# Expert weights in fewer, larger transfers: four slots of 4 MB in place of eight of 2 MB

## The chip, the core and the metric

The kernel runs on one core of a Trainium2 chip. The metric is the device time of one execution in microseconds; it was 1150.12 us before the change (median of three runs, 1147.99 to 1150.42). All data is float32.

## What is computed

One layer of a decoder trunk on 304 tokens (256 prompt tokens behind 16 meta tokens, and 8 sequences of 4 tokens). A mixer of three head groups comes first, then a mixture of 32 experts, of which each token uses four. Both parts end in a layer norm. The change lies in the experts:

```python
def moe(h, lp):
    logits = (xf @ lp["router_w"] + lp["router_b"]).astype(jnp.float32)
    top_val, top_idx = lax.top_k(logits, TOP_K)            # 4 of 32
    gates = jax.nn.softmax(top_val, axis=-1)
    ...
    def expert_block(args):
        xb, e = args
        hid = xb @ lp["moe_w1"][e] + lp["moe_b1"][e]       # 1024 x 2048 weights, 8 MB
        gate = jnp.minimum(hid[:, :D_FF], SWIGLU_LIMIT)
        lin = jnp.clip(hid[:, D_FF:], -SWIGLU_LIMIT, SWIGLU_LIMIT)
        act = gate * jax.nn.sigmoid(SWIGLU_ALPHA * gate) * (lin + 1.0)
        return act @ lp["moe_w2"][e] + lp["moe_b2"][e]     # 1024 x 1024 weights, 4 MB
    ...
    y = jax.ops.segment_sum(rows, tok, num_segments=n)     # sum with the gates
```

Every expert's weights are read once, 32 x 12 MB = 403 MB of the 424 MB that the kernel reads.

## The kernel before

The mixer runs first, up to about 200 us. Its weights and its tensors lie in one large SBUF tensor, `ring`. Its first 32768 columns are afterwards the ring of expert weights: eight slots (`SLOTS`) of 4096 columns (`SLOT`), 16 KB per partition and 2 MB each. An expert is six pieces (`PIECES`): four of the first layer (`W1P`), each 256 rows of `moe_w1`, and two of the second, each 512 rows of `moe_w2`. In both, one partition's share of a piece is one run of 16 KB in memory: partition p holds rows 2p and 2p+1 of a first-layer piece, or rows 4p to 4p+3 of a second-layer piece. Piece number k of the whole sequence goes to slot k mod 8.

All loads of weights are issued by SyncE (SP) in the order of its program. `load_first` loads the pieces of expert 0's first layer while the mixer still runs; each waits with `filled(sp, freed_by(...))` for the last matmul job that reads the mixer's projection weights in that part of the ring. Between them SP issues the second half of `w_out` and, behind them, the rows of the layer norm (`lnbc`). Then come two pieces of expert 1 in the last slots, and the second layer of expert 0 in slots 4 and 5 when job P11 has read `w_out`, which lies there. With that the ring holds eight pieces, 16 MB. From then on `load_group` (L461 to L475) waits before each load until the slot's old piece has been used (`w_used`), which is counted over all pieces.

TensorE takes the experts in pairs. For an expert of the pair (j is 0 or 1) the first layer is eight blocks k of 128 rows (L1651 to L1664). The tokens are the stationary operand, at most 64 per expert, and the weights are the moving one: four products of 512 columns per block, each two matmul instructions in float32. `slot_of` waits for the piece of a block to have landed (`w_full`), and `w_used` is raised after each piece's last block. In the first expert of a pair half of the gather for the following pair is done ahead of block 3 (`gather(1)`), the other half (`gather(0)`) behind the second expert's first layer. The gather picks the tokens of an expert with matmuls (L1610); its stationary operand is `xt` with a step of two columns, because partition p of a piece holds rows 2p and 2p+1. Behind the first layer come the combine of the pair before (L1618, L1625), the transposes of the activation (L1677), the biases of the next expert (L1565) and the second layer, eight blocks again (L1688 to L1700). VectorE and ScalarE compute the activation and add up the results.

Of the kernel before, what the change touches and what calls it, by code (L numbers as in the profile page):

```python
# [22 lines left out]
P = 128  # L23
D = 1024
# [28 lines left out]
C_Z = C_R + DC  # L53
DIN = C_Z + RANK

PIECES = 6
W1P = 4
SLOTS = 8
GROUP = 4
SLOT = 4096  # L60
MB1 = 2048
CAP = 64
PASSES = -(-TOUT // CAP)
# [44 lines left out]
def build_kernel(nc, x_prompt, x_sample, state_conv_a, state_rglru, state_conv_b, state_gla, meta_tokens, ln0_g, ln0_b,  # L108
# [4 lines left out]
    with ExitStack() as ctx:  # L113
# [11 lines left out]
        xt = sb("xt", [P, 3, D])  # L125
# [140 lines left out]
        pick = part("moe", 3, 2 * CAP)  # L266
# [39 lines left out]
        ld_moe = sem("ld_moe")  # L306
        w_full = [sem(f"w_full{s}") for s in range(SLOTS)]
        w_used = sem("w_used")
# [59 lines left out]
            return 64 * (h % 2), h // 2  # L368

        def w1_piece(e, s):  # L370
            return moe_w1[0, bass.ds(e, 1), s * 2 * P:(s + 1) * 2 * P, :].rearrange("a (p t) c -> p (a t c)", t=2)

        def w2_piece(e, s):
            r = (s - W1P) * 4 * P
            return moe_w2[0, bass.ds(e, 1), r:r + 4 * P, :].rearrange("a (p t) c -> p (a t c)", t=4)

        def slot(s):
            return ring[:, s * SLOT:(s + 1) * SLOT]


        @block.sync
        def _(sp):
# [33 lines left out]
            sp.dma_start(wout[:, 0:4, :], w_out[0, 0:4 * P, :].rearrange("(k p) n -> p k n", p=P)).then_inc(ld_wout[0], 16)  # L416
            w1_order = sorted(range(W1P), key=lambda s: J[freed_by(s * SLOT, (s + 1) * SLOT)])

            def load_first(s):
                filled(sp, freed_by(s * SLOT, (s + 1) * SLOT))  # L420
                sp.dma_start(slot(s), moe_w1[0, 0, s * 2 * P:(s + 1) * 2 * P, :].rearrange("(p t) c -> p (t c)", t=2)
                             ).then_inc(w_full[s], 16)

            for s in w1_order[0:3]:
                load_first(s)
            sp.wait_ge(ya_ready, MA)
            sp.wait_ge(outcols_ready, 2)
            sp.dma_start(wout[:, 4:8, :], w_out[0, 4 * P:8 * P, :].rearrange("(k p) n -> p k n", p=P)).then_inc(ld_wout[1], 16)
            for s in w1_order[3:4]:
                load_first(s)  # L430
            sp.wait_ge(h0_ready, 3)
            sp.dma_start(lnbc[:, 0, :], ln1_g.to_broadcast([P, D])).then_inc(ld_ln, 16)
# [4 lines left out]
            sp.wait_ge(S0_decayed, 2)  # L437
            copied(sp, "ST1")
            for s in range(PIECES, SLOTS):
                r = (s - PIECES) * 2 * P  # L440
                sp.dma_start(slot(s), moe_w1[0, 1, r:r + 2 * P, :].rearrange("(p t) c -> p (t c)", t=2)
                             ).then_inc(w_full[s], 16)
            sp.wait_ge(moe_cleared, 4)
            for b in range(2):
# [1 line left out]
                             ).then_inc(ld_moe, 16)  # L446
            sp.dma_start(eout[0:NE, :, :], moe_b2[0].rearrange("e (h c) -> e h c", h=2)).then_inc(ld_moe, 16)
            filled(sp, "P11")
            for s in range(W1P, PIECES):
                r = (s - W1P) * 4 * P  # L450
                sp.dma_start(slot(s), moe_w2[0, 0, r:r + 4 * P, :].rearrange("(p t) c -> p (t c)", t=4)
                             ).then_inc(w_full[s], 16)
            sp.wait_ge(h1_ready, 3)
            sp.dma_start(lnbc[:, 0, :], ln2_g.to_broadcast([P, D])).then_inc(ld_ln, 16)
            sp.dma_start(lnbc[:, 1, :], ln2_b.to_broadcast([P, D])).then_inc(ld_ln, 16)
# [5 lines left out]
            def load_group(e, n, first=0):  # L461

                for i in range(GROUP):
                    if (i + 1) * PIECES <= first:
                        continue
                    ei = e + i if isinstance(e, int) else sp.snap(e + i)
                    for c in range(PIECES):
                        k = i * PIECES + c
                        if k < first:
                            continue  # L470
                        s = k % SLOTS
                        src = w1_piece(ei, c) if c < W1P else w2_piece(ei, c)
                        dst = slot(s)
                        sp.wait_ge(w_used, PIECES * n + k - SLOTS + 1)
                        sp.dma_start(dst, src).then_inc(w_full[s], 16)  # L475

# [822 lines left out]
        def _(pe):  # L1299
# [299 lines left out]
            for t in range(3):  # L1599
                ins = pe.matmul(bank[4][:, 0:NE], ones[:, :], M[:, t, :], start=t == 0, stop=t == 2)  # L1600
# [3 lines left out]
            def gather(half):  # L1604

                for k in range(4 * half, 4 * half + 4):
                    out = bank[(2, 5)[k // 4]][:, (k % 4) * 2 * CAP:(k % 4 + 1) * 2 * CAP]
                    c = 2 * P * (k // 2) + k % 2
                    for t in range(3):
                        ins = pe.matmul(out, xt[:, t, c:2 * P * (k // 2 + 1):2], pick[:, t, :], start=t == 0, stop=t == 2)  # L1610
                ins.then_inc(gather_full, 1)

            def combine(pi, c):
# [17 lines left out]
            for t in range(3):  # L1631
                ins = pe.transpose(bank[3][0:NE, t * P:(t + 1) * P], gates[:, t, :], ident[:, :])
# [3 lines left out]
            with pe.Fori(0, n_pass) as r:  # L1636
                with pe.Fori(0, NE // GROUP) as g:
                    uses = (r * (NE // GROUP) + g) * (GROUP * PIECES // SLOTS)
                    for q in range(2):
                        pi = r * PAIRS + 2 * g + q  # L1640
                        for j in range(2):
                            n = 2 * pi + j

                            def slot_of(c):

                                k = (2 * q + j) * PIECES + c
                                pe.wait_ge(w_full[k % SLOTS], 16 * (uses + k // SLOTS + 1))
                                return k % SLOTS * SLOT


                            for k in range(KT):  # L1651
                                if j == 0 and k == 3:
                                    gather(1)
                                if j == 0 and k % 4 == 0:
                                    pe.wait_ge(xT_ready, 2 * pi + 1 + k // 4)
                                if k % 2 == 0:
                                    at_ = slot_of(k // 2)
                                for b in range(2):
                                    for h in range(2):
                                        c = at_ + k % 2 * MB1 + (2 * b + h) * 512  # L1660
                                        ins = pe.matmul(bank[b][64 * h:64 * h + 64, :], xT[:, q, k, j * CAP:(j + 1) * CAP],  # L1661
                                                        ring[:, c:c + 512], start=False, stop=k == KT - 1)
                                if k % 2 == 1:
                                    ins.then_inc(w_used, 1)  # L1664

                            if j == 1:
# [9 lines left out]
                            for k in range(4):  # L1676
                                ins = pe.transpose(bank[3][:, k * P:(k + 1) * P], l1[:, k:512:4], ident[:, :])  # L1677
# [4 lines left out]
                            if j == 1:  # L1682
                                pe.wait_ge(put_ready, n + 1)
                                for t in range(3):
                                    ins = pe.transpose(bank[3][:, t * P:(t + 1) * P], put[:, t, :], ident[:, :])
                                ins.then_inc(putT_full, 1)
                                pe.wait_ge(out_ready, 2 * n + 1)
                            for k in range(KT):  # L1688
                                if j == 0 and k == 6:
                                    combine(pi, NCOMB - 1)  # L1690
                                if k % 4 == 0:
                                    at_ = slot_of(W1P + k // 4)
                                for h in range(2):
                                    c = at_ + k % 4 * D + h * 512

                                    a = actT[:, k % 4, (k // 4) * CAP:(k // 4 + 1) * CAP]
                                    ins = pe.matmul(bank[4][64 * h:64 * h + 64, :], a, ring[:, c:c + 512],  # L1697
                                                    start=k == 0, stop=k == KT - 1)
                                if k % 4 == 3:
                                    ins.then_inc(w_used, 1)  # L1700

            pe.wait_ge(putT_ready, n_pass * PAIRS + 1)
            pe.wait_ge(out_ready, n_pass * (4 * PAIRS) + 1)
# [31 lines left out]
```

## Time and profile before

| | |
|---|---|
| median of the runs | 1150.12 us (1147.99 to 1150.42) |
| profiled execution, its time | 1150.01 us |
| its span | 1148.2 us |
| TensorE busy | 1089.9 us, 95% of the span |
| DMA: bytes, mean rate | 425.72 MB, 371 GB/s |
| loads of expert weights issued | 192 of 2048 KB, median 31.5 us from issue to landing |

The page gives busy shares of the whole span and a strip of 40 slices. The strip shows the mixer up to slice 7 (about 200 us) with the DMA engines partly idle, and from slice 9 to slice 38 a constant rate of 426 to 429 GB/s. The instructions' rows name engine, line, operation, the tiles written and read, and the shape. PE is the matmul, PEld the load of the stationary operand, SPq the queue of SyncE.

### The profile page before, as it was taken

How to read it: one execution, taken by the hardware profiler on the slowest of the kernel's cores; microseconds unless marked ns; L12 is line 12 of the kernel's file. 1: busy time of each engine (PE TensorE's matmuls, PEld its weight loads, DVE VectorE, ACT ScalarE, POOL GpSimd, SP SyncE). 2: the span in 40 equal slices, each digit the busy share in tenths (PEclk: the TensorE clock that was granted, in tenths of full speed). 3: DMA queues.
4: the chain of work that ended last, by engine and by line, in shares of the span. 5: the costliest groups of instructions: out<-in, count | busy, mean ns of one | idle time of the engine just before them, and what ended most of it. 6: DMA issues, size and time to landing. Idle time of an engine off the chain costs nothing.

```text
span 1148.2 us, 13702 instructions
## 1 busy us (share of the span) xinstructions
PE 1089.9 (95%) x5399; PEld 477.7 (42%) x5399; DVE 341.0 (30%) x798; ACT 166.2 (14%) x290; POOL 73.5 (6%) x119
## 2 busy tenths in 40 slices
PE   6999899999999999999999999999999999999994
PEld 3666536534444434434344333333333333333331
DVE  3489755322121212121212121212121212121225
ACT  3444122110111011101010101011101110110002
POOL 8401430000000000000000000000000000000000
PEclk9999888899999999999999999999999999999997
DMA  9522845599999999999999999999999999999991
GB/s 311 168 74 74 336 174 197 212 399 428 426 428 428 429 429 429 428 428 429 429 428 429 429 428 428 429 429 429 428 428 428 429 429 428 429 429 428 428 420 44
DMA packets 40700, 425.72 MB, mean 371 GB/s; under 512 B 7073, under 2 KB 11302, under 8 KB 16097
## 3 DMA queue, kind: packets, MB, share of 16 engines
q1 hardware_dynamic: 38761, 423.68, 88.3%
q0 software_dynamic: 1920, 1.80, 0.6%
q8 instruction: 11, 0.18, 0.1%
q14 instruction: 8, 0.07, 0.0%
HBM read 423.50 MB, written 2.17 MB: 371 GB/s over the span
## 4 chain that ended last, share of the span: by engine, by line
PE 68%; DMA 25%; DVE 5%; ACT 1%; issue 1%; SPq 0%; ACTq 0%; DVEq 0%
PE bank L1661 25%; DMA ring<-in_moe_w_dram 25%; PE bank L1697 14%; PE bank L1314 8%; PE bank L1610 7%; PE bank L1625 5%; PE bank L1565 2%; PE bank L1349 1%; PE bank L1677 1%; PE bank L1618 1%; PE bank L1530 1%; DVE ring L1001 1%; PE bank L1395 0%; PE bank L1319 0%; DVE stat L870 0%
## 5 line engine op out<-in xcount | busy, mean ns | idle before, releaser
L1661 PE MATMUL bank<-ring,hT 128*64 128x512 f32 x2048 | 454.2, 594 | 20.4 <-DMA ring<-in_moe_w_dram 19.7
L1661 PEld LDWEIGHTS bank<-ring,hT 128*64 128x64 f32 x2048 | 143.0, 137 | 313.6 <-issue 262.8
L1697 PE MATMUL bank<-ring 128*64 128x512 f32 x1024 | 230.3, 597 | 0.0
L1268 DVE TENSOR_SCALAR ring<-bank 128x512 f32<-128x512 f32 x32 | 22.1, 692 | 372.6 <-PE bank L1661 372.6
L1697 PEld LDWEIGHTS bank<-ring 128*64 128x64 f32 x1024 | 69.2, 137 | 146.6 <-issue 140.1
L1610 PEld LDWEIGHTS bank<-ring,xt 128*128 128x128 f32 x792 | 98.1, 201 | 27.9 <-issue 26.0
L1610 PE MATMUL bank<-ring,xt 128*128 128x128 f32 x792 | 104.3, 290 | 1.8 <-DVE ring L1200 1.8
L1206 DVE COPY hT<-bank 128x512 f32<-128x512 f32 x33 | 22.6, 684 | 258.9 <-PE bank L1610 258.9
L842 ACT ACTIVATE ring<-ring 128x512 f32<-128x512 f32 x32 | 20.2, 630 | 491.5 <-DVE ring L1268 491.5
L851 ACT ACTIVATE ring<-bank 64x512 f32<-64x512 f32 x64 | 37.8, 591 | 243.9 <-PE bank L1697 243.1
L1217 DVE TENSOR_TENSOR ring<-ring,bank 128x512 f32<-128x512 f32 x68 | 43.4, 676 | 87.9 <-PE bank L1625 87.8
L1625 PE MATMUL bank<-ring 128*128 128x512 f32 x136 | 67.2, 617 | 0.0
L648 POOL TENSOR_TENSOR ring<-ring 128x256 f32<-128x256 f32 x1 | 0.7, 719 | 962.2 <-ACT ring L857 962.2
L1314 PE MATMUL bank<-hT,ring 128*128 128x304 f32 (+2 forms) x176 | 47.3, 430 | 3.5 <-DVE hT L904 2.5
L1314 PEld LDWEIGHTS bank<-hT,ring 128*128 128x128 f32 (+1 forms) x176 | 32.2, 184 | 17.9 <-issue 7.6
L1625 PEld LDWEIGHTS bank<-ring 128*128 128x128 f32 x136 | 23.1, 189 | 36.7 <-issue 36.7
L1565 PE MATMUL bank<-ring 32*64 32x512 f32 x264 | 35.9, 613 | 0.0
L1314 PE MATMUL bank<-ring 128*128 128x512 f32 (+1 forms) x92 | 35.3, 542 | 0.0
L1001 DVE SCALAR_TENSOR_TENSOR ring<-ring 128x256 f32<-128x256 f32 x60 | 32.8, 588 | 1.1
L844 ACT ACTIVATE ring<-bank 128x512 f32<-128x512 f32 x32 | 19.1, 597 | 74.8 <-PE bank L1677 74.8
L1314 PEld LDWEIGHTS bank<-ring 128*128 128x128 f32 x92 | 17.3, 190 | 17.0 <-issue 14.9
L1277 DVE TENSOR_SCALAR ring<-io,ring 128x64 f32<-128x64 f32 x96 | 23.9, 300 | 0.0
(290 smaller groups left out, 621.1 us busy)
## 6 DMA issues: line engine op xcount, KB each, us to landing
ring<-in_moe_w_dram SPq DMA_DIRECT2D x192, 2048.0 KB, 31.5
ring<-in_w_out_dram SPq DMA_DIRECT2D x2, 2048.0 KB, 12.2
ring<-in_w_in_dram SPq DMA_DIRECT2D x2, 1536.0 KB, 17.1
ring<-in_w_in_dram SPq DMA_DIRECT2D x1, 3072.0 KB, 24.8
ring<-in_w_in_dram SPq DMA_DIRECT2D x1, 2048.0 KB, 13.6
ring<-in_w_in_dram SPq DMA_DIRECT2D x1, 1600.0 KB, 8.1
lnbc<-in_ln_g_dram SPq DMA_DIRECT2D x3, 512.0 KB, 20.9
lnbc<-in_ln_b_dram SPq DMA_DIRECT2D x3, 512.0 KB, 11.2
```

The costliest lines, as they stand in the source:

```text
L851: act.activation(eout[64 * j:64 * j + 64, h, :], bank[4][64 * h:64 * h + 64, :], ACT.Copy).then_inc(out_ready, 1)
L1001: st.do(dve.scalar_tensor_tensor(uc[:, m, 0:SEQ], src, w, uc[:, m, 0:SEQ], ALU.mult, ALU.add), uc_ready if (k, m) == (WB - 1, MB - 1) else ...
L1206: dve.tensor_copy(xT[:, parity, 4 * b:4 * b + 4, :], bank[(2, 5)[b]][:, :].rearrange("p (k c) -> p k c", c=2 * CAP)).then_inc(xT_ready, 1)
L1217: dve.tensor_tensor(dst, dst, bank[COMB_BANK[c]][:, :], ALU.add).then_inc(y_added, 1)
L1268: dve.tensor_scalar(g1[:, :], bank[0][:, :], LIMIT, None, ALU.min).then_inc(g1_ready, 1)
L1277: ins = dve.tensor_scalar(put[:, t, j * CAP:(j + 1) * CAP], io64[:, :], posm[:, t, bass.ds(n, 1)], gates[:, t, bass.ds(e, 1)], ALU.is_equa ...
L1314: ins = pe.matmul(out, a, b, start=n == 0, stop=n == len(pairs) - 1)
L1565: pe.matmul(bank[b][64 * h:64 * h + 64, :], bsel[e0:e0 + NE, j, :], b1_sb[e0:e0 + NE, h, :], start=True, stop=False)
L1610: ins = pe.matmul(out, xt[:, t, c:2 * P * (k // 2 + 1):2], pick[:, t, :], start=t == 0, stop=t == 2)
L1625: pe.matmul(out[:, :], putT[:, t * P:(t + 1) * P], eout[:, h, :], start=True, stop=True).then_inc(comb_full, 1)
L1661: ins = pe.matmul(bank[b][64 * h:64 * h + 64, :], xT[:, q, k, j * CAP:(j + 1) * CAP], ring[:, c:c + 512], start=False, stop=k == KT - 1)
L1697: ins = pe.matmul(bank[4][64 * h:64 * h + 64, :], a, ring[:, c:c + 512], start=k == 0, stop=k == KT - 1)
```

## The change

An expert is now three pieces of 4 MB: two of the first layer, 512 rows each, and one second layer. The ring has four slots of 8192 columns. In a piece of the first layer partition p holds rows 4p to 4p+3, one run of 32 KB in memory. A second layer is loaded in one transfer with two runs of 16 KB per partition, one from each half. The order of rows in the first layer is another, so the gather's stationary operand is read with a step of four columns. Waits for landing and signals of use follow the larger pieces.

```diff
--- before.py
+++ after.py
@@ -53,11 +53,11 @@
 C_Z = C_R + DC
 DIN = C_Z + RANK
 
-PIECES = 6
-W1P = 4
-SLOTS = 8
+PIECES = 3
+W1P = 2
+SLOTS = 4
 GROUP = 4
-SLOT = 4096
+SLOT = 8192
 MB1 = 2048
 CAP = 64
 PASSES = -(-TOUT // CAP)
@@ -368,11 +368,10 @@
             return 64 * (h % 2), h // 2
 
         def w1_piece(e, s):
-            return moe_w1[0, bass.ds(e, 1), s * 2 * P:(s + 1) * 2 * P, :].rearrange("a (p t) c -> p (a t c)", t=2)
-
-        def w2_piece(e, s):
-            r = (s - W1P) * 4 * P
-            return moe_w2[0, bass.ds(e, 1), r:r + 4 * P, :].rearrange("a (p t) c -> p (a t c)", t=4)
+            return moe_w1[0, bass.ds(e, 1), s * 4 * P:(s + 1) * 4 * P, :].rearrange("a (p t) c -> p (a t c)", t=4)
+
+        def w2_piece(e):
+            return moe_w2[0, bass.ds(e, 1), :, :].rearrange("a (h p t) c -> p (a h) (t c)", h=2, t=4)
 
         def slot(s):
             return ring[:, s * SLOT:(s + 1) * SLOT]
@@ -418,15 +417,15 @@
 
             def load_first(s):
                 filled(sp, freed_by(s * SLOT, (s + 1) * SLOT))
-                sp.dma_start(slot(s), moe_w1[0, 0, s * 2 * P:(s + 1) * 2 * P, :].rearrange("(p t) c -> p (t c)", t=2)
+                sp.dma_start(slot(s), moe_w1[0, 0, s * 4 * P:(s + 1) * 4 * P, :].rearrange("(p t) c -> p (t c)", t=4)
                              ).then_inc(w_full[s], 16)
 
-            for s in w1_order[0:3]:
+            for s in w1_order[0:1]:
                 load_first(s)
             sp.wait_ge(ya_ready, MA)
             sp.wait_ge(outcols_ready, 2)
             sp.dma_start(wout[:, 4:8, :], w_out[0, 4 * P:8 * P, :].rearrange("(k p) n -> p k n", p=P)).then_inc(ld_wout[1], 16)
-            for s in w1_order[3:4]:
+            for s in w1_order[1:2]:
                 load_first(s)
             sp.wait_ge(h0_ready, 3)
             sp.dma_start(lnbc[:, 0, :], ln1_g.to_broadcast([P, D])).then_inc(ld_ln, 16)
@@ -437,8 +436,8 @@
             sp.wait_ge(S0_decayed, 2)
             copied(sp, "ST1")
             for s in range(PIECES, SLOTS):
-                r = (s - PIECES) * 2 * P
-                sp.dma_start(slot(s), moe_w1[0, 1, r:r + 2 * P, :].rearrange("(p t) c -> p (t c)", t=2)
+                r = (s - PIECES) * 4 * P
+                sp.dma_start(slot(s), moe_w1[0, 1, r:r + 4 * P, :].rearrange("(p t) c -> p (t c)", t=4)
                              ).then_inc(w_full[s], 16)
             sp.wait_ge(moe_cleared, 4)
             for b in range(2):
@@ -446,10 +445,8 @@
                              ).then_inc(ld_moe, 16)
             sp.dma_start(eout[0:NE, :, :], moe_b2[0].rearrange("e (h c) -> e h c", h=2)).then_inc(ld_moe, 16)
             filled(sp, "P11")
-            for s in range(W1P, PIECES):
-                r = (s - W1P) * 4 * P
-                sp.dma_start(slot(s), moe_w2[0, 0, r:r + 4 * P, :].rearrange("(p t) c -> p (t c)", t=4)
-                             ).then_inc(w_full[s], 16)
+            sp.dma_start(slot(W1P).rearrange("p (h c) -> p h c", h=2), moe_w2[0, 0].rearrange("(h p t) c -> p h (t c)", h=2, t=4)
+                         ).then_inc(w_full[W1P], 16)
             sp.wait_ge(h1_ready, 3)
             sp.dma_start(lnbc[:, 0, :], ln2_g.to_broadcast([P, D])).then_inc(ld_ln, 16)
             sp.dma_start(lnbc[:, 1, :], ln2_b.to_broadcast([P, D])).then_inc(ld_ln, 16)
@@ -469,8 +466,8 @@
                         if k < first:
                             continue
                         s = k % SLOTS
-                        src = w1_piece(ei, c) if c < W1P else w2_piece(ei, c)
-                        dst = slot(s)
+                        src = w1_piece(ei, c) if c < W1P else w2_piece(ei)
+                        dst = slot(s) if c < W1P else slot(s).rearrange("p (h c) -> p h c", h=2)
                         sp.wait_ge(w_used, PIECES * n + k - SLOTS + 1)
                         sp.dma_start(dst, src).then_inc(w_full[s], 16)
 
@@ -1605,9 +1602,9 @@
 
                 for k in range(4 * half, 4 * half + 4):
                     out = bank[(2, 5)[k // 4]][:, (k % 4) * 2 * CAP:(k % 4 + 1) * 2 * CAP]
-                    c = 2 * P * (k // 2) + k % 2
+                    c = 4 * P * (k // 4) + k % 4
                     for t in range(3):
-                        ins = pe.matmul(out, xt[:, t, c:2 * P * (k // 2 + 1):2], pick[:, t, :], start=t == 0, stop=t == 2)
+                        ins = pe.matmul(out, xt[:, t, c:4 * P * (k // 4 + 1):4], pick[:, t, :], start=t == 0, stop=t == 2)
                 ins.then_inc(gather_full, 1)
 
             def combine(pi, c):
@@ -1653,14 +1650,14 @@
                                     gather(1)
                                 if j == 0 and k % 4 == 0:
                                     pe.wait_ge(xT_ready, 2 * pi + 1 + k // 4)
-                                if k % 2 == 0:
-                                    at_ = slot_of(k // 2)
+                                if k % 4 == 0:
+                                    at_ = slot_of(k // 4)
                                 for b in range(2):
                                     for h in range(2):
-                                        c = at_ + k % 2 * MB1 + (2 * b + h) * 512
+                                        c = at_ + k % 4 * MB1 + (2 * b + h) * 512
                                         ins = pe.matmul(bank[b][64 * h:64 * h + 64, :], xT[:, q, k, j * CAP:(j + 1) * CAP],
                                                         ring[:, c:c + 512], start=False, stop=k == KT - 1)
-                                if k % 2 == 1:
+                                if k % 4 == 3:
                                     ins.then_inc(w_used, 1)
 
                             if j == 1:
@@ -1688,16 +1685,15 @@
                             for k in range(KT):
                                 if j == 0 and k == 6:
                                     combine(pi, NCOMB - 1)
-                                if k % 4 == 0:
-                                    at_ = slot_of(W1P + k // 4)
+                                if k == 0:
+                                    at_ = slot_of(W1P)
                                 for h in range(2):
-                                    c = at_ + k % 4 * D + h * 512
+                                    c = at_ + k * D + h * 512
 
                                     a = actT[:, k % 4, (k // 4) * CAP:(k // 4 + 1) * CAP]
                                     ins = pe.matmul(bank[4][64 * h:64 * h + 64, :], a, ring[:, c:c + 512],
                                                     start=k == 0, stop=k == KT - 1)
-                                if k % 4 == 3:
-                                    ins.then_inc(w_used, 1)
+                            ins.then_inc(w_used, 1)
 
             pe.wait_ge(putT_ready, n_pass * PAIRS + 1)
             pe.wait_ge(out_ready, n_pass * (4 * PAIRS) + 1)
```

## Rows read from the trace of the kernel before

**Rows 1.** the page: busy time, and the chain that ended last, by engine
```profile
PE 1089.9 (95%) x5399; PEld 477.7 (42%) x5399; DVE 341.0 (30%) x798; ACT 166.2 (14%) x290; POOL 73.5 (6%) x119
...
PE 68%; DMA 25%; DVE 5%; ACT 1%; issue 1%; SPq 0%; ACTq 0%; DVEq 0%
```

**Rows 2.** stretches: us, busy PE, PEld, DVE, ACT, POOL, clock, DMA share, GB/s
```profile
213.00:214.00 1.00, 1.00 (x8) 0.21 (x4) 0.00 (x0) 0.00 (x0) 0.00 (x0) 1.00 1.22 229
...
213.00:250.00 37.00, 37.00 (x184) 14.23 (x182) 7.97 (x20) 2.41 (x4) 0.00 (x0) 1.00 0.94 368
...
500.00:600.00 100.00, 100.00 (x504) 39.59 (x502) 22.47 (x51) 10.85 (x18) 0.00 (x0) 1.00 1.01 429
...
600.00:700.00 100.00, 96.77 (x479) 37.31 (x475) 20.05 (x49) 10.06 (x16) 0.00 (x0) 1.00 1.01 428
```

**Rows 3.** timeline of TensorE, two pairs' first lines: start, us, line, operation, count
```profile
543.85 5.32 PE L1661 MATMUL bank<-ring,hT 128*64 128x512 f32 x24
...
573.82 13.90 PE L1661 MATMUL bank<-ring,hT 128*64 128x512 f32 x64
...
599.65 0.60 PE L1661 MATMUL bank<-ring,hT 128*64 128x512 f32 x2
```

**Rows 4.** DMA view of 73 to 75 us (4 KiB runs) and 300 to 1100
```profile
DMA packets 202, 0.83 MB, mean 414 GB/s; under 512 B 0, under 2 KB 0, under 8 KB 202
...
q1 hardware_dynamic: 202, 0.83, 102.5%
...
DMA packets 23536, 342.74 MB, mean 428 GB/s; under 512 B 2617, under 2 KB 2617, under 8 KB 2617
...
q1 hardware_dynamic: 23534, 342.71, 100.6%
```

**Rows 5.** waits of TensorE on weights: total, times, longest
```profile
PE bank L1661 <- DMA ring<-in_moe_w_dram: 19.7, 26, 1.2
```

**Rows 6.** timeline of TensorE at the start of the stream
```profile
209.00 5.37 PE L1661 MATMUL bank<-ring,hT 128*64 128x512 f32 x24 [0.69 <-DVE hT L1206]
...
214.30 3.09 PE L1610 MATMUL bank<-ring,xt 128*128 128x128 f32 x24
...
217.33 8.80 PE L1661 MATMUL bank<-ring,hT 128*64 128x512 f32 x40
...
237.25 1.94 PE L1697 MATMUL bank<-ring 128*64 128x512 f32 x8
```

**Rows 7.** timeline of SP's queue: start, us, line, tile, count
```profile
105.34 14.07 SPq L421 DMA_DIRECT2D ring<-in_moe_w_dram  x3
...
119.53 0.38 SPq L428 DMA_DIRECT2D ring<-in_w_out_dram  x1
...
212.69 40.60 SPq L475 DMA_DIRECT2D ring<-in_moe_w_dram  x10
```

**Rows 8.** timeline of TensorE at the end of the stream
```profile
1106.84 3.65 PE L1661 MATMUL bank<-ring,hT 128*64 128x512 f32 x16 [0.64 <-DMA ring<-in_moe_w_dram]
...
1111.73 3.65 PE L1661 MATMUL bank<-ring,hT 128*64 128x512 f32 x16 [1.24 <-DMA ring<-in_moe_w_dram]
...
1115.32 3.09 PE L1610 MATMUL bank<-ring,xt 128*128 128x128 f32 x24
...
1120.40 7.09 PE L1697 MATMUL bank<-ring 128*64 128x512 f32 x32
```

**Rows 9.** weight loads by line: ns min/median/max, first and last start
```profile
L1610 PEld LDWEIGHTS bank<-ring,xt x792: 192/197/331, 202.6 to 1118.0; 128*128 128x128 f32 x198
...
L1677 PEld LDWEIGHTS bank<-ident,ring x128: 195/209/222, 229.0 to 1118.6; 128*128 128x128 f32 x128
...
L1685 PEld LDWEIGHTS bank<-ident,ring x48: 137/140/143, 257.5 to 1120.1; 128*128 128x128 f32 x48
```

**Rows 10.** timelines of TensorE, VectorE: first uses of w_out, of the norm's rows
```profile
145.45 9.18 PE L1530 MATMUL bank<-ring 128*64 128x512 f32 x32
...
160.81 1.26 DVE L886 SCALAR_TENSOR_TENSOR xt<-xt,mv,lnbc 32x1024 f32<-32x1024 f32 x1
```

## Prediction

> **What bounds the kernel now.** I read the page first: the matmul engine is busy 95% of the span, and the chain that ended last lies 68% on it and 25% on the loads of expert weights [rows 1]. Both numbers are averages over two regimes, so I read the table of stretches next. Between 500 and 600 us TensorE has no idle time at all; between 600 and 700 it is idle for 3.2%; the DMA engines move 428 to 429 GB/s in both [rows 2]. The stream of weights is saturated from about 240 us to the end, and only the lead changes: at 209 us the ring holds 16 MB, TensorE eats a pair of experts in 55.80 us (543.85 to 599.65) [rows 3], and the stream delivers one in 12 transfers of 2 MiB at 342.74 MB in 800 us, 428.4 GB/s [rows 4], 12 x 4.895 = 58.74 us. TensorE gains 2.9 us per pair, so the lead is used up near 600 us. From there it waits for weights, 19.7 us in 26 waits, all in the first layer of an expert [rows 5]. So the end of the kernel is: first issue of the stream, plus what the stream loses at its start, plus the bytes at the stream's rate, plus what TensorE does after the last first-layer transfer has landed. Each edit is costed in these four terms.
>
> **The start of the stream.** Loads are issued when a slot has been used. Before, slot 0 is used after two of eight row blocks (k): the first matmuls start at 209.00 [rows 6], SP issues at 212.69 [rows 7]. After, it is used after four, and between the third and the fourth lies the second half of the gather (214.30, 3.09 us). The fourth block is 8 of the 40 matmuls that take 8.80 us from 217.33 [rows 6], so it ends at 217.33 + 1.76 = 219.09; with the 0.1 us that lay between use and issue before, the first issue is at 219.2, 6.5 us later. Not all of it is lost. Before, the queue ran dry between the small slots: 368 GB/s over the stretch 213 to 250 [rows 2], 13.6 MB. After, traffic begins about 1 us behind the issue (before, 229 GB/s between 213 and 214 is half of the full rate, so traffic began near 213.5 to 213.7) [rows 2], so at 220.2. Two transfers of 4 MiB keep it busy until 220.2 + 2 x 9.79 = 239.8. The second slot is free at 226.2 (the 40 matmuls end at 226.13), in time. The third slot, the whole second layer, is free when its last matmuls end at 237.25 + 1.94 = 239.2 [rows 6], and its load arrives at 240.3: a gap of 0.5 us. The fourth is free 7.04 us later at 246, the next at 253, the one after that when expert 1 ends, 25.83 us after its start (573.82 to 599.65) [rows 3], so at 265; the stream would want them at 250, 260 and 270. So 29.3 us of traffic by 250, 12.55 MB, against 13.6: 1.05 MB or 2.5 us behind. I add 0.5 us for the ramp of the first transfer: **+3.0 us**. Bounds: +2.5 if there is no ramp, +6.5 if none of the old gaps is won back.
>
> **In the steady part** the ring is as large as before (16 MB), so a load waits for a slot only if TensorE is late. A matmul of the first layer takes 0.22 us of TensorE's time (8.80 / 40) [rows 6], four blocks 7.04, an odd expert 25.83 and an even one 55.80 - 25.83 = 29.97 [rows 3]. Transfers of 4 MiB land 9.73 us apart. Count from the landing A of an even expert's first piece: it is used at A + 7.04 + 3.09 = A + 10.1, the second (landed A + 9.7) at A + 17.2, and the expert ends at A + 30.0. The odd one has used its first piece at A + 37.0, waits for the second until A + 38.9, and needs the other 25.83 - 7.04 = 18.8 us from there, so it ends at A + 57.7, before the next pair's first landing at A + 58.4. A piece is used 7 to 11 us after its landing, and the stream wants the slot 27 us after it. So the stream stays saturated, and TensorE waits 2 to 3 us per pair, in fewer and longer waits of up to 1.9 us.
>
> **The rate of the stream.** The one gain. First-layer transfers change from 16 KiB runs to 32 KiB runs; the second layer keeps 16 KiB runs (two per partition). The trace before has no load with 32 KiB runs, so I draw a line through two sizes. With 4 KiB runs (the load of w_out, alone on the queue) it moves 414 GB/s, 4096 x 16 / 414 = 158.3 ns per run and engine; with 16 KiB runs 428.4 GB/s, 611.9 ns [rows 4]. The slope is 453.6 / 12288 = 36.9 ps per byte, which leaves 7.1 ns fixed per run. By the shares of busy time instead (102.5% of 16 engines x 2 us / 202 runs = 162.4 ns; 100.6% x 16 x 800 us / 20,919 long runs = 615.6 ns, less a little for the short packets) it is near 11 [rows 4]. I take 8, nearer the first, because shares over 100% count overlap. 92 transfers follow after the prefetch, 61 of the first layer; each of these saves 8 runs per engine, 488 in all, and 92 of the short packets that end a transfer vanish (2617 short packets in 800 us, 16 per transfer [rows 4]), which I count like a fixed part. 580 x 8 ns = **-4.6 us**. Bounds: 0 and 580 x 11 = -6.4.
>
> The Trainium skill, DMA: Bandwidth & Descriptors, section on where 436 GB/s comes from, puts the limit of the ports at 435.2 GB/s. The slope above is 434 GB/s over 16 engines, so the trace agrees. At that limit the 256 MB of the first layer would go 9.3 us faster, an end that no run length can pass.
>
> **The end.** The last transfer of the first layer lands one second layer's worth (4 MiB, 9.8 us) before the stream ends, as before. Then TensorE worked off two blocks (1111.73 to 1115.32, 3.6 us); now it has four, 7.04 us: +3.45 us. Behind it nothing moves: gather, transposes and biases until the second layer at 1120.40, 5.1 us [rows 8]. The second layer is now waited for whole, but it lands 9.8 us after the first layer's last piece and is wanted 12 us after it, so that wait is hidden; it would cost 3.5 us if the first layer were faster than 4.7 us there.
>
> **The gather** now reads its stationary operand with a step of 16 bytes, before 8. The transposes of line 1677 read theirs with 16 already: median weight load 209 ns, against 197 in the gather and 140 for the contiguous ones of line 1685 [rows 9]. 24 loads x 12 ns is at most 0.3 us per half gather; as the loads overlap matmuls I take 0.1, once in the tail: **+3.55 us** for the end together. In the steady part it hides in the 2.9 us of slack per pair.
>
> The Trainium skill, SBUF — State Buffer, note on cachelines, says that accesses which each cross to a new 16-byte line pay a penalty. The rows show one, of 12 ns. What a doubled load would do is a rival below.
>
> **The preload** costs nothing that I can find. Before, one 2 MiB slot was filled from 105.34 [rows 7]; now slot 0 waits for the same projection as the others and is issued near 119. w_out's second half goes out behind the same 4 MiB as before (119.53) [rows 7] and is needed at 145.45 [rows 10]. The last 4 MiB and the norm's rows, some 30 us of transfers from 119 on, land 2 MiB or 4.9 us later, near 150; the first use of those rows is at 160.81 [rows 10]. SP's issues halve in number; none waits behind something new, since SP took the slots in the same order before.
>
> **Sum.** 3.0 + 3.55 - 4.6 = +1.95 us. The profiled run took 1150.01 us (span 1148.2 and 1.8 around it), 0.1 under the median of 1150.12, so the forecast is **1152.0 us**.
>
> **Rivals.** (A) Runs of 32 KiB save nothing: they are cut, or the fixed part goes by bytes. Only the short packets are saved, 0.7 us: 3.0 + 3.55 - 0.7 = +5.9, 1156.0 us. For it: no row has such a run. Against: the step from 4 to 16 KiB did save. (B) The other side, faster: the fixed part is larger than the line says, because 16 KiB runs hide some of it under load. It decides the sign where 580 runs x fixed = 6.55 us, at 11.3 ns, the value from shares; from 15.3 ns on the kernel is measurably faster, 1147.7 us. For it: the share above 100%; against: the rates give 7.1. (C) TensorE becomes the bound in the gather. If each strided load took another 140 ns on the path, a pair would take 55.8 + 2 x 24 x 0.14 = 62.5 us, over 58.4, and 15.5 pairs from 239 us end near 1208: about 1231 us. Line 1677 speaks against. The skill's cacheline rule, read strictly, would be this case. (D) The ring of four slots starves the stream while TensorE is the slower one (before 600 us): a second layer frees 4 MiB at once and late. It decides from the point at which a slot is freed later than the stream wants it; above, that holds once (0.5 us) and the next margins are 4 to 7 us. One microsecond at each of five pairs would give 1157 us.
>
> **Chances.** Forecast 0.57 (1150.5 to 1154), A 0.20, B 0.14, C 0.03, D 0.06. The range leaves out C and the far ends of A, B and D: 1148.8 to 1157.0 us. A measurement of this kernel can tell about 0.2% (2.3 us) from no change. The forecast lies just inside that, so its case is split, 0.33 same and 0.22 slower, 0.02 faster; with A, C and D slower and B two thirds faster: faster 0.12, same 0.38, slower 0.50.
>
> **What would show it.** First weight issue in the loop near 219.2 instead of 212.7; GB/s of 213 to 250 near 335; GB/s of 300 to 1100 near 430.5 (A: 428.7, B: over 432); 8,192 packets of 16 KiB and 8,192 of 32 KiB for the 24,576 of 16 KiB; TensorE's waits on weights longer than 1.24 us and fewer; from the last wait to the second layer 12.2 instead of 8.7 us. The prediction is wrong if the stream shows slices under 428 GB/s between 250 and 1100 us, if the granted clock falls there, or if the half gather takes over 3.4 us.

## The result, and the profile after

The changed kernel takes 1212.49 us (median; 1211.54 to 1212.77), against 1150.27 us of the kernel before on the same chip: a ratio of 1.0544, 95% interval 1.0531 to 1.0556. That is 62 us slower, where 2 were forecast, and outside the range.

The page of the kernel after says where to look. First its busy line, the granted clock and the rate in 40 slices, and the chain that ended last, by engine and by line (line numbers are three lower than before: L1607 is the gather, L1658 the first layer, L1674 the transposes):

```profile
PE 1172.0 (97%) x5399; PEld 568.0 (47%) x5399; DVE 342.5 (28%) x798; ACT 166.3 (14%) x290; POOL 73.6 (6%) x119
...
PEclk9999797999999999999999999999999999999997
...
GB/s 305 149 70 18 371 178 183 250 421 403 420 388 425 405 426 399 421 398 425 398 425 398 419 398 426 392 429 399 419 401 424 405 417 399 429 398 419 398 174 39
...
PE 93%; DVE 5%; ACT 1%; issue 1%; DMA 0%; ACTq 0%; DVEq 0%
...
PE bank L1658 37%; PE bank L1694 19%; PE bank L1607 16%; PE bank L1311 8%; PE bank L1622 5%; PE bank L1562 3%; PE bank L1346 1%; PE bank L1674 1%; PE bank L1615 1%; PE bank L1527 1%; DVE ring L998 1%; PE bank L1682 1%; PE bank L1392 0%; PE bank L1316 0%; DVE stat L867 0%
```

The chain was 68% TensorE and 25% DMA [rows 1]; now DMA has gone from it. As many instructions run on TensorE as before (5399), but their loads of stationary operands are 90 us longer in sum (568.0 against 477.7). The rate, a flat 428 to 429 GB/s before [rows 2], swings between 388 and 429, and a load of expert weights lands 15.2 us after its issue (median), where it took 31.5. So fewer loads stand ready in the queue: the stream now waits for slots, that is, for TensorE.

The stretches of the kernel after (columns as in [rows 2]) show TensorE without a pause for 800 us, where it was idle for 3.2% between 600 and 700 us [rows 2], and at full clock:

```profile
213.00:250.00 37.00, 37.00 (x170) 16.09 (x168) 7.98 (x20) 2.41 (x4) 0.00 (x0) 1.00 0.72 294
...
300.00:1100.00 800.00, 800.00 (x3695) 366.41 (x3693) 158.87 (x378) 78.06 (x124) 0.00 (x0) 1.00 0.98 411
```

And the timeline of TensorE names the work that grew. These lines answer to [rows 3] and [rows 6]:

```profile
209.92 5.37 PE L1658 MATMUL bank<-ring,hT 128*64 128x512 f32 x24 [0.69 <-DVE hT L1203]
...
271.22 5.32 PE L1658 MATMUL bank<-ring,hT 128*64 128x512 f32 x24
276.47 5.87 PE L1607 MATMUL bank<-ring,xt 128*128 128x128 f32 x24
282.26 8.80 PE L1658 MATMUL bank<-ring,hT 128*64 128x512 f32 x40
...
332.47 5.32 PE L1658 MATMUL bank<-ring,hT 128*64 128x512 f32 x24
...
1183.00 7.09 PE L1694 MATMUL bank<-ring 128*64 128x512 f32 x32
```

Half a gather takes 5.87 us where it took 3.09 [rows 6]; everything else on TensorE has its old duration. A pair of experts takes 332.47 - 271.22 = 61.25 us, against 55.80 [rows 3]: 2 x 2.78 = 5.56 us more, less 0.1 us that the transposes behind the half gather are shorter. Sixteen such pairs from 209.92 end at 1189.9, and the last second layer ends at 1183.00 + 7.09 = 1190.1. The whole of the time lies in that product. The weight loads by line (columns as in [rows 9]) hold the cause:

```profile
L1607 PEld LDWEIGHTS bank<-ring,xt x792: 307/330/330, 203.0 to 1180.6; 128*128 128x128 f32 x198
...
L1674 PEld LDWEIGHTS bank<-ident,ring x128: 195/209/300, 232.7 to 1181.2; 128*128 128x128 f32 x128
```

A weight load of the gather takes 330 ns with a step of four columns. It took 197 ns with a step of two, and the transposes with a step of four still take 209 [rows 9].

### The profile page after: what moved, and what is told of

Same layout as the page of the kernel before. It is cut to its first block, busy times and chain, and to the rows that moved or that the text cites. A ratio compares the mean times of both kernels' runs of the same rounds, so it can differ in the third digit from the quotient of the medians.

```text
span 1210.8 us, 13354 instructions
## 1 busy us (share of the span) xinstructions
PE 1172.0 (97%) x5399; PEld 568.0 (47%) x5399; DVE 342.5 (28%) x798; ACT 166.3 (14%) x290; POOL 73.6 (6%) x119
## 4 chain that ended last, share of the span: by engine, by line
PE 93%; DVE 5%; ACT 1%; issue 1%; DMA 0%; ACTq 0%; DVEq 0%
PE bank L1658 37%; PE bank L1694 19%; PE bank L1607 16%; PE bank L1311 8%; PE bank L1622 5%; PE bank L1562 3%; PE bank L1346 1%; PE bank L1674 1%; PE bank L1615 1%; PE bank L1527 1%; DVE ring L998 1%; PE bank L1682 1%; PE bank L1392 0%; PE bank L1316 0%; DVE stat L867 0%
## 5 line engine op out<-in xcount | busy, mean ns | idle before, releaser
L1658 PE MATMUL bank<-ring,hT 128*64 128x512 f32 x2048 | 448.5, 593 | 0.7 <-DVE hT L1203 0.7
L1658 PEld LDWEIGHTS bank<-ring,hT 128*64 128x64 f32 x2048 | 145.5, 137 | 285.6 <-issue 283.7
L1607 PEld LDWEIGHTS bank<-ring,xt 128*128 128x128 f32 x792 | 187.3, 329 | 27.9 <-issue 26.0
L1607 PE MATMUL bank<-ring,xt 128*128 128x128 f32 x792 | 193.6, 402 | 1.8 <-DVE ring L1197 1.8
L1674 PEld LDWEIGHTS bank<-ident,ring 128*128 128x128 f32 x128 | 21.0, 217 | 7.5 <-DVE ring L1271 5.3
## 6 DMA issues: line engine op xcount, KB each, us to landing
ring<-in_moe_w_dram SPq DMA_DIRECT2D x96, 4096.0 KB, 15.2
```

Of the source, the lines that this page charges most:

```text
L1607: ins = pe.matmul(out, xt[:, t, c:4 * P * (k // 4 + 1):4], pick[:, t, :], start=t == 0, stop=t == 2)
```

## The experiments

**The step of the gather alone, and the change without it.** Theory G: the strided weight loads of the gather are the whole loss. Rival S: the larger pieces, or four slots in place of eight, starve TensorE or the stream. The first kernel is the one before with one edit:

```diff
-                    c = 2 * P * (k // 2) + k % 2
+                    c = 4 * P * (k // 4) + k % 4
                     for t in range(3):
-                        ins = pe.matmul(out, xt[:, t, c:2 * P * (k // 2 + 1):2], pick[:, t, :], start=t == 0, stop=t == 2)
+                        ins = pe.matmul(out, xt[:, t, c:4 * P * (k // 4 + 1):4], pick[:, t, :], start=t == 0, stop=t == 2)
```

> The kernel before with one edit: the gather reads its stationary operand with a step of four columns, as the changed kernel does. Pieces, ring and transfers stay as they were. The edit picks columns in another order than the pieces of weights hold their rows, so the products are of wrong pairs; the amount of work is the same. Theory G (the step of the gather's weight loads is the whole loss): weight loads of the gather 330 ns, half a gather 5.9 us, a pair of experts 61.3 us, no waits of TensorE on weights, about 1212 us. Rival S (the larger pieces or the smaller number of slots starve TensorE or the stream): the step costs little, 1150 to 1153 us.

Measured: 1212.86 us, ratio 1.0558 (1.0541 to 1.0574), the time of the changed kernel. Its span is 1210.8 us, as that one's. As expected, its weight loads take 330 ns and half a gather 5.87 us, and TensorE has no wait on expert weights. The second kernel is the changed one with these lines turned back:

```diff
-                    c = 4 * P * (k // 4) + k % 4
+                    c = 2 * P * (k // 2) + k % 2
                     for t in range(3):
-                        ins = pe.matmul(out, xt[:, t, c:4 * P * (k // 4 + 1):4], pick[:, t, :], start=t == 0, stop=t == 2)
+                        ins = pe.matmul(out, xt[:, t, c:2 * P * (k // 2 + 1):2], pick[:, t, :], start=t == 0, stop=t == 2)
```

> The changed kernel with one edit: the gather reads with a step of two columns, as before (wrong columns for the new order of rows, so the products are of wrong pairs; the amount of work is the same). Theory G: the rest of the sum in the prediction holds, 1152.0 us; first issue in the loop near 219.2, rate of 300 to 1100 us near 430.5 GB/s, TensorE waits for weights again from some 550 us on, up to 2 us at a time; if 32 KiB runs save nothing, 1156 us. Rival S: stays above 1200 us.

Measured: 1152.4 us, ratio 1.0023 (1.0014 to 1.0032). So G holds from both sides, and S falls. What is left of the change is 2.6 us by this ratio, where 1.95 was forecast. The profile of this kernel has the signs that the prediction named: TensorE's first block and SP's queue, the stretches, the DMA view of 300 to 1100 us, the waits on weights, and TensorE from its first long wait to the end:

```profile
208.45 5.37 PE L1658 MATMUL bank<-ring,hT 128*64 128x512 f32 x24 [0.69 <-DVE hT L1203]
...
218.75 34.03 SPq L472 DMA_DIRECT2D ring<-in_moe_w_dram  x5
```

```profile
213.00:250.00 37.00, 37.00 (x182) 14.18 (x180) 7.97 (x20) 2.41 (x4) 0.00 (x0) 1.00 0.82 338
```

```profile
DMA packets 15288, 344.52 MB, mean 431 GB/s; under 512 B 1315, under 2 KB 1315, under 8 KB 1315
```

```profile
PE bank L1658 <- DMA ring<-in_moe_w_dram: 24.2, 22, 1.9
```

```profile
527.04 7.09 PE L1658 MATMUL bank<-ring,hT 128*64 128x512 f32 x32 [1.78 <-DMA ring<-in_moe_w_dram]
...
1111.46 7.09 PE L1658 MATMUL bank<-ring,hT 128*64 128x512 f32 x32 [1.80 <-DMA ring<-in_moe_w_dram]
1118.48 3.09 PE L1607 MATMUL bank<-ring,xt 128*128 128x128 f32 x24
...
1123.57 7.09 PE L1694 MATMUL bank<-ring 128*64 128x512 f32 x32
```

**Runs of 32 KB against two of 16 KB.** The third kernel has the same pieces of 4 MB and four slots, but the first layer is loaded as the second: two runs of 16 KB per partition. The gather's step is then two by right. The core of the edit (the preloads change in the same way):

```diff
-            return moe_w1[0, bass.ds(e, 1), s * 4 * P:(s + 1) * 4 * P, :].rearrange("a (p t) c -> p (a t c)", t=4)
+            return moe_w1[0, bass.ds(e, 1), s * 4 * P:(s + 1) * 4 * P, :].rearrange("a (h p t) c -> p (a h) (t c)", h=2, t=2)
...
-                        dst = slot(s) if c < W1P else slot(s).rearrange("p (h c) -> p h c", h=2)
+                        dst = slot(s).rearrange("p (h c) -> p h c", h=2)
```

> The changed kernel with transfers of 4 MB whose partitions hold two runs of 16 KB in the first layer too (rows 2p and 2p+1 of each half), so the gather's step is two again and everything is computed. Theory G with the rate as predicted: 1.95 + 488 x 8 ns = 5.9 us over before, 1156 us, and 3.9 us more than with runs of 32 KB; rate of 300 to 1100 us near 428.7 GB/s. If runs of 32 KB save nothing, the same time as with them. Rival S: above 1200 us.

Measured: 1157.51 us, ratio 1.0067 (1.0054 to 1.0080). The DMA view of 300 to 1100 us:

```profile
DMA packets 22233, 342.77 MB, mean 428 GB/s; under 512 B 1312, under 2 KB 1312, under 8 KB 1312
```

342.77 MB against 344.52 in the same 800 us is 428.5 against 430.7 GB/s, a difference of 0.51%. TensorE's waits for pieces say the same. In the kernel with runs of 32 KB ten pairs lie between the landings at 527.04 and 1111.46, 58.44 us each. Here they lie between 528.32 and 1115.70, 58.74 us each:

```profile
209.86 5.37 PE L1658 MATMUL bank<-ring,hT 128*64 128x512 f32 x24 [0.52 <-DVE hT L1203]
...
220.16 34.02 SPq L472 DMA_DIRECT2D ring<-in_moe_w_dram  x5
...
528.32 7.09 PE L1658 MATMUL bank<-ring,hT 128*64 128x512 f32 x32 [2.02 <-DMA ring<-in_moe_w_dram]
...
587.08 8.78 PE L1658 MATMUL bank<-ring,hT 128*64 128x512 f32 x32 [2.13 <-DMA ring<-in_moe_w_dram]
...
880.78 8.78 PE L1658 MATMUL bank<-ring,hT 128*64 128x512 f32 x32 [2.01 <-DMA ring<-in_moe_w_dram]
...
1115.70 8.79 PE L1658 MATMUL bank<-ring,hT 128*64 128x512 f32 x32 [2.01 <-DMA ring<-in_moe_w_dram]
```

A pair has 32 runs fewer per engine with runs of 32 KB, so a run saved is worth about 9 ns (0.30 us / 32), where 8 were taken. So the runs of 32 KB do save. Not all of it reached the end, though. At 0.51% the stream's 900 us would be 4.6 us shorter, and 3.9 were expected; but from the first issue to the landing of the last first-layer piece the two profiles take 892.71 us (218.75 to 1111.46) and 895.54 (220.16 to 1115.70), only 2.8 us apart. At the first long waits, 308.3 and 308.2 us behind the first issue, no gain had reached TensorE yet. Why the first 300 us show no gain stays open.

The profiled execution of this kernel has a span 5.9 us longer than that of the kernel with runs of 32 KB: 1.4 us because TensorE's first block starts later (209.86 against 208.45), the 2.8 us of the stream, and 1.7 us for another reason. Its TensorE waited 2.01 us for the last first-layer piece, and the stretch behind the wait had the granted clock at 0.68, between the two levels of 2.4 and 1.2 GHz:

```profile
1115.70:1121.00 5.30, 5.30 (x18) 1.72 (x20) 0.00 (x0) 0.00 (x0) 0.00 (x0) 0.68 0.99 420
```

Its four blocks took 8.79 us there, not 7.09. The lines above show the same behind two earlier waits, at 587.08 and 880.78 (clock 0.65 and 0.67 over the 5 us behind them), where the next wait for weights took it up. Six other waits of 2.0 to 2.1 us in this profile were followed by four blocks in 7.09 us, at full clock, and so were all eleven waits of 1.8 to 1.9 us in the kernel with runs of 32 KB. The mean granted clock was 0.974 to 0.975 in all five executions of this kernel, and 0.977 to 0.982 in the eleven of the other, so such dips are probably in all five. Whether one always falls on the last wait, where it costs time, is not known.

**How the price goes with the step.** Three kernels, each the one before with another step in the gather (the new lines side by side, with the columns that each reads behind them):

```diff
+                    c = P * k                               # step 1: xt[:, t, c:c + P]
+                    c = 3 * P * (k % 2) + k // 2            # step 3: xt[:, t, c:c + 3 * P:3]
+                    c = k                                   # step 8: xt[:, t, c:8 * P:8]
```

> The kernel before with the gather reading 128 adjacent columns (step one; wrong columns for the order of rows, same work). If the price of a weight load starts only at a step of 16 bytes, the loads take 189 ns, like the contiguous loads of line 1625, half a gather 3.0 us, and the time stays that of before (TensorE has slack). If step two already costs on the path, half a gather falls well under 3 us; the time stays the same even so, because the weights' stream sets it.

> The same with a step of three columns (12 bytes). Theory L (the load pays for each new 16-byte line it touches): 128 columns touch 96 lines, so the load lies three quarters of the way from step one to step four, near 290 ns, half a gather 5 us. Rival D (a limit at 16 bytes: free below, full price from there): as step two, 197 ns and 3.1 us, 1150 us.

> The same with a step of eight columns (32 bytes). Both theories: the same as step four, 330 ns, half a gather 5.9 us, 1212 us, since each column lies in a line of its own with either. Rival: the price goes with the distance, then over 400 ns and over 1230 us.

The weight loads of the gather in the three, in that order (ns, min/median/max):

```profile
L1610 PEld LDWEIGHTS bank<-ring,xt x779: 186/192/333, 204.8 to 1116.5; 128*128 128x128 f32 x195
```

```profile
L1610 PEld LDWEIGHTS bank<-ring,xt x758: 250/262/329, 204.7 to 1095.0; 128*128 128x128 f32 x190
```

```profile
L1610 PEld LDWEIGHTS bank<-ring,xt x738: 312/336/338, 204.7 to 1123.7; 128*128 128x128 f32 x185
```

| step, columns (bytes) | load, median ns | half a gather, us | pair, us | time, us |
|---|---|---|---|---|
| 1 (4) | 192 | 2.94 | 55.7 | 1148.82, ratio 0.999 (0.9981 to 1.0) |
| 2 (8), before | 197 | 3.09 | 55.80 | 1150 |
| 3 (12) | 262 | 4.50 | 58.45 | 1166.88 (one run) |
| 4 (16) | 330 | 5.87 | 61.25 | 1212.86 |
| 8 (32) | 336 | 6.02 | 61.52 | 1217.40 (one run) |

The price rises between steps of 8 and 16 bytes and hardly after. Neither expectation for step three was met: 262 ns is halfway between 192 and 330, not three quarters, and not free. The number of lines touched alone does not fit either: from step one to step two it doubles, from 32 to 64, and the load grows by 5 ns. Halfway is what comes out if a column pays when it is alone on its 16-byte line: with 12 bytes between columns, of each four (0, 12, 24, 36) two share a line and two are alone, so 64 of 128 pay; with 16 all do, with 8 none. It is 1.1 ns per column by step three (70 / 64) and by step four (138 / 128). That fits three points and is a reading, not a test of its own.

The Trainium skill, Advanced Engine Details and Errata, section on memory cachelines, says that at least two accesses must hit a 16-byte line of SBUF for the latency to be absorbed. These rows agree, step three included.

**Why the row I compared with misled.** Line 1677 reads with a step of four and loads in 209 ns. Theory K: its transposes are another kind of instruction, one transposing pass in place of two float32 passes, whose loads are cheaper at any step. Rival P: the place of the tile decides. One kernel writes the transposes as float32 products with the identity, step unchanged:

```diff
-                                ins = pe.transpose(bank[3][:, k * P:(k + 1) * P], l1[:, k:512:4], ident[:, :])
+                                ins = pe.matmul(bank[3][:, k * P:(k + 1) * P], l1[:, k:512:4], ident[:, :], start=True, stop=True)
```

> The kernel before with the four transposes of line 1677 written as float32 products with the identity; their stationary operand keeps its step of four columns. Theory K (the row I compared with was of another kind of instruction, a transposing pass, whose loads are cheaper at every step): the loads of line 1677 rise from 209 ns to about 330 ns and double in number (8 for 4), their pace to about 240 ns. Rival P (the place of the tile decides, xt against the ring): they stay near 209 ns. The time is that of before in both.

The other leaves the transposes and takes their step away:

```diff
-                                ins = pe.transpose(bank[3][:, k * P:(k + 1) * P], l1[:, k:512:4], ident[:, :])
+                                ins = pe.transpose(bank[3][:, k * P:(k + 1) * P], l1[:, k * P:(k + 1) * P], ident[:, :])
```

> The kernel before with the transposes of line 1677 reading adjacent columns (wrong columns for the second layer, same work). Theory K: these are transposing passes, whose contiguous loads take 140 ns, so they fall from 209 to 140 ns; the row that I compared with was itself a slow load, half as long again as its own kind. Rival: they stay near 209 ns, whatever the step. The time stays 1150 us in both.

The loads of line 1677, first as products, then as transposes of adjacent columns:

```profile
L1677 PEld LDWEIGHTS bank<-ident,ring x248: 307/329/332, 229.7 to 1108.2; 128*128 128x128 f32 x124
```

```profile
L1677 PEld LDWEIGHTS bank<-ident,ring x128: 137/141/146, 229.5 to 1119.0; 128*128 128x128 f32 x128
```

The same tile with the same step takes 329 ns as a product and 209 as a transpose; K holds, P falls. Within its own kind the step costs the transpose 68 ns (141 to 209), the product 138. Little of the 68 is paid: the four transposes take 0.73 and 0.64 us in the kernel before, and 0.64 and 0.60 without the step, so 10 to 23 ns each. The time of the second was 1150.47 us (one run), as expected. The time of the first was not: 1167.87 us (one run), where no change was expected. Its eight products take 1.90 to 2.12 us in place of 0.64 to 0.73, a pair takes 58.46 us (502.01 to 560.47), and that was under the stream's 58.74.

**From what point TensorE decides.** This miss, and step three with its 58.45 us and 1166.88, show that the point is lower than the stream's time per pair. Theory M puts it where 16 pairs fill the time from TensorE's start at 209.00 [rows 6] to the end of its last second layer, 1120.40 + 7.09 = 1127.49 [rows 8]: 918.5 / 16 = 57.4 us. A kernel just below it, with a step of four in two of the eight blocks:

```diff
-                    c = 2 * P * (k // 2) + k % 2
+                    c, w = (4 * P + k % 4, 4) if k in (4, 5) else (2 * P * (k // 2) + k % 2, 2)
                     for t in range(3):
-                        ins = pe.matmul(out, xt[:, t, c:2 * P * (k // 2 + 1):2], pick[:, t, :], start=t == 0, stop=t == 2)
+                        ins = pe.matmul(out, xt[:, t, c:c + P * w - w + 1:w], pick[:, t, :], start=t == 0, stop=t == 2)
```

> The kernel before; of the eight blocks of the gather two (k of 4 and 5) read with a step of four columns (wrong columns, same work), the others with two. 12 of 48 loads per pair pay 115 ns more, a pair takes about 57.2 us. Theory M (TensorE sets the end once 16 pairs take longer than from its start at 209 us to the end that the stream sets, 918.5 us, so from 57.4 us per pair on, not from the 58.7 us of the stream): just below the point, no change, 1150 us, with the waits of TensorE on weights down to a few us from some 20. Rival N (every nanosecond of the gather costs time): 1150 + 16 x 1.4 = 1172 us.

Measured: 1150.7 us, ratio 1.0009 (0.9999 to 1.0018). The pair (494.19 to 551.37) takes 57.18 us, and the waits on weights have all but gone:

```profile
494.19 5.32 PE L1661 MATMUL bank<-ring,hT 128*64 128x512 f32 x24
...
551.37 5.32 PE L1661 MATMUL bank<-ring,hT 128*64 128x512 f32 x24
```

```profile
PE bank L1661 <- DMA ring<-in_moe_w_dram: 3.3, 5, 1.1
```

M holds, N falls. Above the point the end follows the product: step three starts its first layer at 208.88, and 208.88 + 16 x 58.45 = 1144.1, where its last second layer ends at 1137.26 + 7.09 = 1144.35.

## Why the prediction was wrong, step by step

**The gather: the step that failed.** The prediction priced the new step by the difference between two rows of [rows 9], 209 ns for line 1677 and 197 for the gather, and took 12 ns. The rows are of two kinds: a transposing pass, whose contiguous load is the 140 ns of line 1685, and a float32 product, whose contiguous load is 189 to 192. Within one kind the same rows said 209 against 140, half as much again. Applied to the gather's 192 that is 287 ns, and by the sum's own form 24 x 0.09 = 2.2 us per half gather; measured were 133 ns per load against step two and 2.78 us. "As the loads overlap matmuls I take 0.1" was wrong for the same reason. In the gather a matmul of 128 columns starts every 0.13 us (3.09 / 24), less than even the old load of 197 ns, so there is no long product for the loads to hide behind, and the longer load is paid nearly in full: 2.78 / 24 = 116 of the 133 ns.

**Rival C was the mechanism, and was given 3%.** It said TensorE becomes the bound in the gather, priced the load at +140 ns (measured +133), a pair at 62.5 us (61.25) and the whole at 1231 us (1212.5). "Line 1677 speaks against" rested on the mismatched pair of rows. The Trainium skill's note on cachelines, which the prediction cites, pointed to this rival, and was set aside for that row. Two of the three signs that the prediction gave for being wrong came with it: slices under 428 GB/s, and a half gather over 3.4 us. The third, a lower granted clock, did not.

**The slack: wrong as well, and it would have hidden a smaller loss.** "It hides in the 2.9 us of slack per pair" set TensorE's 55.80 against the stream's 58.74. But TensorE starts with a full ring, 16 MB of weights for which the stream needs no time later. The experiments put the point at 57.4 us, so the slack is 1.6 us per pair, 0.8 per half gather. Step three lies between the two figures and costs 17 us.

**What the prediction had right,** read in the changed kernel with the old step:

- Start: issue 10.3 us behind TensorE's first block (208.45 to 218.75) against 3.7 before, so 6.6 us later (6.5 predicted); 338 GB/s from 213 to 250 (335).
- Rate: 344.52 MB in 800 us, 430.7 GB/s (430.5). The fixed part of a run, taken as 8 ns (the line through runs of 4 and 16 KB gave 7.1), comes out near 9 at 32 KB.
- Steady part: longest wait 1.9 us (1.9), 22 waits; the stream stays saturated with four slots.
- End: 1111.46 to 1123.57, 12.1 us (12.2).
- Sum: a ratio of 1.0023 is 2.6 us (1.6 to 3.7), predicted 1.95. With runs of 16 KB the ratio of 1.0067 is 7.7 us, predicted 5.9 as rival A; 1.7 us of it may be the clock dip seen in its profile.

That the sum came out so close is in part luck. From TensorE's first block to the last first-layer landing the profile before has 902.73 us (209.00 to 1111.73) and this one 903.01 (208.45 to 1111.46), so start and rate together cost 0.3 us, where 3.0 - 4.6 = -1.6 was forecast. The kernel with two runs splits that. It takes 905.84 us (209.86 to 1115.70), so the start, less the short packets, cost 3.1 us, where 3.0 - 0.7 was forecast, and the long runs gave back 2.8, where 3.9 was forecast. With the 3.4 us of the end this makes 3.7 us, and TensorE's start 0.55 us earlier leaves the 3.2 us between the two spans. These are single profiles, and executions of this kernel spread from 1149.75 to 1153.80 us, so parts of 1 us are not settled by them.

Rivals A, B and D are not what happened. A falls with the pair of kernels above. B would have needed over 11.3 ns per run; it is near 9. D needed a stream that waits for slots with TensorE at its old speed, and its rate is 431 GB/s. In the kernel after the stream does wait, but as an effect of the slow gather.

Without the gather's step the change would lose 2.6 us: larger pieces cost about 3 us at the start and 3.4 at the end, and the runs of 32 KB give back less than that. Nothing here points to a kernel faster than the one before. A copy of `xt` in the pieces' order, which would make the gather contiguous with runs of 32 KB, was not tried; a step of one instead of two was worth 0.1% at most.

## What to carry to other kernels

Reordering the rows of a weight tile for longer transfers moves a stride into whatever feeds the matching operand, so price that side first, and by rows of the same kind of instruction (product with product, transpose with transpose) at both steps. In a run of matmuls that are as short as their weight loads, as the 24 of a half gather here, most of a longer load is paid (116 of 133 ns). Where a kernel starts with a full buffer, the slack of the engine behind it is (end minus its start) / rounds, less than the gap between the two rates, and it can be used up by an edit on the side of the engine that was waiting.

## What the hardware showed that was not expected

- A float32 weight load of 128 x 128 takes 192, 197, 262, 330 and 336 ns with 4, 8, 12, 16 and 32 bytes between columns; a transposing one takes 141 contiguous and 209 with 16.
- Joining two DMA runs of 16 KB per partition to one of 32 KB saves about 9 ns per engine, near the fixed part of 7 to 8 ns read from runs of 4 and 16 KB: 430.7 against 428.5 GB/s with two thirds of the bytes in such runs.
- After three of nine waits of 2.0 to 2.1 us the granted clock stood at 0.65 to 0.68 over the next 5 us; after the other six, and after eleven of 1.8 to 1.9 us in another kernel, four blocks took 7.09 us, as at full clock.
